# Softmax statistics through DMAs, a second stage 14 units behind, and query casts on GpSimd in a three-group attention layer

## What is computed

```python
qa, ka, va, ga, qb, kb, vb, gb, qc, gc = jnp.split(proj, IN_SPLITS, axis=-1)
# A: 6 heads, causal window of 128, a learned sink per head
oa, _ = banded_attention(qa * scale, ka, va, A_WINDOW - 1, sink)
# B: 6 heads, three (window, dilation) pairs, combined by their softmax denominators
for (win, dil) in ((128, 1), (512, 4), (2048, 16)):
    qs = to_strided(qb * scale, dil)[:, :, :, None, :]
    o, lse = banded_attention(qs, to_strided(kb, dil), to_strided(vb, dil), win // dil, None)
    outs.append(from_strided(o[:, :, :, 0], B, dil).astype(jnp.float32))
    lses.append(from_strided(lse[..., 0], B, dil))
wts = jax.nn.softmax(jnp.stack(lses, axis=0), axis=0)
ob = jnp.sum(wts[..., None] * jnp.stack(outs, axis=0), axis=0)
# C: 4 heads, cross attention into 256 memory tokens
pc = jax.nn.softmax(sc, axis=-1)
```

## Time and profile before

| | |
|---|---|
| median of 3 runs | 2151.43 us (2144.21 to 2152.7) |
| profiled execution | 2152.24 us, of it a span of 2150.1 us from the first to the last instruction |
| TensorE, VectorE, ScalarE, GpSimd busy | 95%, 73%, 63%, 5% of the span |
| mean granted clock of TensorE | 0.973 |
| ten rounds of B (1100.04 to 1499.74 us) | 39.97 us each |
| nine rounds of A (1569.85 to 1689.95 us) | 13.34 us each |

### The profile page before, as it was taken

The page is one execution under the profiler, slowest core; times in us unless marked ns, Lnnn a source line. Parts: engine busy times, 40 slices in busy tenths (PEclk is TensorE's granted clock), DMA queues, the critical chain, the costliest instruction groups (busy, mean ns, idle before and its releaser), DMA issues. The chain is left out here.

```text
span 2150.1 us, 39340 instructions
## 1 busy us (share of the span) xinstructions
PE 2040.4 (95%) x12892; PEld 1717.2 (80%) x12892; DVE 1559.2 (73%) x4410; ACT 1352.9 (63%) x3520; POOL 115.9 (5%) x116
## 2 busy tenths in 40 slices
PE   5999999999999999999889999999999998899998
PEld 4787778888888888888778888887888887688886
DVE  6564674546654574436589999989799997888886
ACT  7454454544555464343699999989699997533333
POOL 1232310000000000002100000000000000000000
PEclk7999999999999999999889999999999999999999
DMA  4466576777577667588876687686779895345543
GB/s 158 152 229 222 177 242 180 217 247 217 155 223 212 225 196 235 184 286 272 201 148 138 130 167 143 131 161 139 150 184 220 227 249 171 98 164 168 176 160 113
DMA packets 351736, 401.40 MB, mean 187 GB/s; under 512 B 105616, under 2 KB 255248, under 8 KB 346688
## 3 DMA queue, kind: packets, MB, share of 16 engines
q1 hardware_dynamic: 343120, 364.80, 62.0%
q0 software_dynamic: 8432, 34.30, 5.2%
HBM read 255.62 MB, written 143.39 MB: 186 GB/s over the span
## 5 line engine op out<-in xcount | busy, mean ns | idle before, releaser
L854 PE MATMUL p_ps<-p_u_hi,p_w_hi 128*128 128x512 f32 x1344 | 534.0, 397 | 26.7 <-DVE p_p_c L739 10.8
L856 PE MATMUL p_ps<-p_u_hi,p_w_lo 128*128 128x512 f32 x1344 | 526.6, 392 | 0.0
L855 PE MATMUL p_ps<-p_u_lo,p_w_hi 128*128 128x512 f32 x1344 | 525.6, 391 | 0.0
L570 DVE TENSOR_TENSOR p_w_lo<-p_w_raw,p_w_hi 128x512 fp32r<-128x512 f32 x336 | 246.6, 734 | 327.0 <-ACT p_w_hi L423 325.4
L1621 ACT ACTIVATE probs<-probs,a_stat 128x256 f32<-128x256 f32 (+1 forms) x896 | 437.4, 497 | 38.9 <-DVE a_stat L1455 36.5
L423 ACT ACTIVATE p_w_hi<-p_w_raw 128x512 fp32r<-128x512 f32 x336 | 211.2, 629 | 329.0 <-PE p_ps L856 304.7
L854 PEld LDWEIGHTS p_ps<-p_u_hi,p_w_hi 128*128 128x128 f32 x1344 | 254.2, 189 | 85.4 <-issue 13.0
L856 PEld LDWEIGHTS p_ps<-p_u_hi,p_w_lo 128*128 128x128 f32 x1344 | 253.7, 189 | 54.4
L855 PEld LDWEIGHTS p_ps<-p_u_lo,p_w_hi 128*128 128x128 f32 x1344 | 254.2, 189 | 50.8
L1455 DVE CUSTOM_DVE_ANT_0 probs<-a_ps_s,fixed 128x256 f32<-128x256 f32 (+1 forms) x704 | 251.9, 398 | 48.3 <-PE a_ps_s L1354 45.7
L1424 PE MATMUL a_ps_t<-fixed,probs 128*128 128x128 f32 x1660 | 262.0, 279 | 23.6 <-ACT a_pT L1645 16.5
(11 more groups left out here) (202 smaller groups left out, 2762.6 us busy)
## 6 DMA issues: line engine op xcount, KB each, us to landing
p_w_raw<-in_w_in SPq DMA_DIRECT2D x156, 256.0 KB, 3.7
p_w_raw<-scratch_w_s SPq DMA_DIRECT2D x144, 256.0 KB, 3.6
scratch_qk_hi<-p_out_a SPq DMA_DIRECT2D x80, 256.0 KB, 4.0
scratch_qk_lo<-p_out_b SPq DMA_DIRECT2D x80, 256.0 KB, 4.1
a_v<-scratch_v SPq DMA_DIRECT2D x40, 512.0 KB, 8.2
scratch_gate<-p_out_a SPq DMA_DIRECT2D x64, 256.0 KB, 3.8
scratch_v<-p_out_a SPq DMA_DIRECT2D x256, 64.0 KB, 2.3
a_gate<-scratch_gate SPq DMA_DIRECT2D x64, 256.0 KB, 6.0
```

The source lines that it names most:

```text
L570: nc.vector.tensor_tensor(w_lo[:, m % 3, :, :], w_raw[:, entry(j, g), :, :], w_hi[:, m % 3, :, :].bitcast(F32), ALU.subtract).then_inc(w_l ...
L854: nc.tensor.matmul(bank, hi, u_hi[j][:, k, :], start=j < 2 and k == 0, stop=False, skip_group_check=True)
L855: nc.tensor.matmul(bank, hi, u_lo[j][:, k, :], start=False, stop=False, skip_group_check=True)
L856: last = nc.tensor.matmul(bank, lo, u_hi[j][:, k, :], start=False, stop=k == KH - 1, skip_group_check=True)
```

## The change

- `TAIL` of B is 14 instead of 18. The exchange stands earlier in the round: slots 1 to 5 and 9, with the far spread in slot 9 and its small matmuls in slot 11 of the round before.
- The statistics of the middle units go another way: GpSimd stores them to DRAM as soon as pair 19 has its sums, waits, and loads them back in four DMAs in the layout that VectorE needs. The middle weights go back the same way. Eight of the eleven small matmuls of a phase and VectorE's four picking instructions are gone. Dependent steps of VectorE stand at different places of a slot, with work between them.
- GpSimd makes all casts: eight in a phase of B, four in one of A. VectorE and ScalarE make none.
- Group A reads its sink without a copy.

```diff
-        return Unit("r4", (c, r), (n, r), P * len(tiles), tiles, r, 16 + 4 * c + r)
+        return Unit("r4", (c, r), (n, r), P * len(tiles), tiles, r, 16 + 4 * r + c)
...
-    TAIL = 18 if kind == "B" else 4
+    TAIL = 14 if kind == "B" else 4
...
-                for b in range(NCH):
-                    last = nc.tensor.matmul(ps_x[:, 128 + 32 * b:160 + 32 * b].rearrange("p (x n) -> p x n", x=2), group4[:, b, :],
-                                            stat[:, s, :, 16:32], start=True, stop=True)
...
-            if kind == "A" and slot == 0:
-                dve.nop(nofuse=True)
-                nc.vector.tensor_copy(sink_now[:, s, :], sink[:, :, bass.ds(h, 1)].rearrange(
-                    "p a o -> p (a o)")).then_inc(sink_ready, 1)
-                dve.wait_ge(sink_ready, p + 1)
...
+            if at == (2, 0):
+                dve.wait_ge(step, done + 1)
+                dve.wait_ge(middle_loaded, 64 * p + 64)
+                nc.vector.tensor_tensor(by_chunk(low), middle[:, 0, :, :], by_chunk(work[:, 0, 0:16]), ALU.min).then_inc(step, 1)
...
+            if kind == "B" and e == 8:
+                dve.wait_ge(middle_back, 64 * p + 64)
...
+    def pool_parts(pool):
+
+        def gather(phase):
+
+            p, s = number(phase), phase[1]
+            pool.wait_ge(sums_ready, p * NP + 20)
+            pool.dma_start(sc["middle_stats"], stat[:, s, 32:64]).then_inc(middle_stored, 16)
+            pool.wait_ge(middle_stored, 32 * p + 16)
+            for b in range(NCH):
+                pool.dma_start(middles[:, 8 * b:8 * b + 8],
+                               sc["middle_stats"][32 * b:32 * b + 32, :].rearrange("j (r e) -> r j e", r=NCH)).then_inc(middle_loaded, 16)
+
+        def give_back(phase):
+
+            p, s = number(phase), phase[1]
+            pool.wait_ge(weights_ready, p + 1)
+            pool.dma_start(sc["middle_weights"], work[:, 7, 16:32]).then_inc(middle_stored, 16)
+            pool.wait_ge(middle_stored, 32 * p + 32)
+            for r in range(NCH):
+                pool.dma_start(coef[:, s, 16 + 4 * r:20 + 4 * r],
+                               sc["middle_weights"][32 * r:32 * r + 32, :].rearrange("j (b c) -> b j c", c=NCH)).then_inc(middle_back, 16)
+
+        def cast(phase):
+
+            p = number(phase)
+            if kind == "B" and p > 0:
+                pool.wait_ge(q_loaded, 32 * p)
+                pool.wait_ge(scores_ready, p * NP)
+                for i in range(4):
+                    nc.gpsimd.tensor_copy(q[:, 1, i * CHUNK:(i + 1) * CHUNK].rearrange("p (b i a) -> p b i a", i=4, a=8),
+                                          by_residue(q[:, 0, :])[:, 4 * i:4 * i + 4, :].rearrange(
+                                              "p i (b a) -> p b i a", a=8).bitcast(F32)).then_inc(q_copied, 1)
+                for g in range(4):
+                    nc.gpsimd.tensor_copy(*natural_piece(g)).then_inc(natural_copied, 1)
...
+        def pool_round(a, c, b, d):
+            if a and a.g.kind == "B":
+                a.parts.cast(a.phase)
+                if c:
+                    c.parts.give_back(c.phase)
+                a.parts.gather(a.phase)
+            elif a and a.g.kind == "A":
+                n = 2 * a.phase[0] + a.phase[1]
+                if n == 0:
+                    a.parts.cast((0, 0))
+                    c.parts.give_back(c.phase)
+                a.parts.cast(((n + 1) // 2, (n + 1) % 2))
```

More of the change, by code:

```diff
@@ L1453, in scores @@
                 a = 2 * P - u.keys
-                start = sink_now[:, s, 1:2] if kind == "A" else 3e38
+                start = sink[:, 1, h:h + 1] if kind == "A" else 3e38
                 last = nc.vector.tensor_tensor_reduce(
@@ new lines, in exchange @@
+            at = (slot, place)
+            done = p * DVE_STEPS
+            far = ps_x[:, 0:32].rearrange("p (x b) -> p x b", x=2)
+            middle = middles.rearrange("p (b x c) -> p x c b", x=2, c=NCH)
+            by_chunk = lambda of: of.rearrange("p (c b) -> p c b", b=NCH)
+            low, ex, inv = work[:, 1, 0:16], work[:, 3, :], work[:, 6, 0:16]
+            if at == (1, 2):
+                dve.wait_ge(max_ready, p * NP + NP)
+                dve.wait_ge(gathered, p + 1)
+                nc.vector.tensor_tensor(work[:, 0, 0:16], far[:, 0, :], near_stat(s, 0), ALU.min).then_inc(step, 1)
@@ L1675, in scalar_parts @@
-        return named(scores=scores, exchange=exchange, copy=copy, keep=keep, copy_queries=copy_queries)
+        return named(scores=scores, exchange=exchange, copy=copy, keep=keep)
+    def pool_parts(pool):
[8 more added lines that the diff above has]
+        def give_back(phase):
+            p, s = number(phase), phase[1]
+            pool.wait_ge(weights_ready, p + 1)
[5 more added lines that the diff above has]
+        def cast(phase):
+            p = number(phase)
+            if kind == "B" and p > 0:
[7 more added lines that the diff above has]
+                    nc.gpsimd.tensor_copy(*natural_piece(g)).then_inc(natural_copied, 1)
+            if kind == "A" and p < 2 * heads:
+                pool.wait_ge(q_loaded, 32 * p + 32)
+                if p < 2:
+                    pool.wait_ge(prev.scores_ready, prev.TOTAL)
+                else:
+                    pool.wait_ge(scores_ready, (p - 1) * NP)
+                for g in range(4):
+                    nc.gpsimd.tensor_copy(*natural_part(p, g)).then_inc(q_copied, 1)
+        return named(gather=gather, give_back=give_back, cast=cast)
@@ L1751, in tensor_round @@
                 if c:
-                    c.parts.exchange(c.phase, i)
+                    c.parts.give_back(c.phase, i)
+                for v in slot.new:
+                    a.parts.gather(a.phase, v)
                 if slot.two_before and slot.two_before[1] % 2:
@@ L1758, in vector_round @@
             for i, slot in enumerate(slots_of(a, c, b, d)):
-                if c and c.g.kind != "B":
-                    c.parts.exchange(c.phase, i)
+                if c:
+                    c.parts.exchange(c.phase, i, 0)
                 if slot.ahead:
@@ L1776, in vector_round @@
                     x.parts.gated(x.phase, e)
-                if c and c.g.kind == "B":
-                    c.parts.exchange(c.phase, i)
+                if c:
+                    c.parts.exchange(c.phase, i, 2)
+                for v in slot.new:
+                    a.parts.spread_far(a.phase, v)
         def scalar_round(a, c, b, d):
```

216 lines of the change are left out of this document (81 added, 135 removed).

## The result

The changed kernel takes 2172.3 us (median of 4 runs, 2170.43 to 2173.61) against 2148.57 for the kernel before in the same session: a ratio of 1.011, 95% interval 1.0084 to 1.0136. It is slower, by 24 us; the forecast was 2135. The profiled execution has a span of 2169.6 us, 19.5 above that of before.

A forecast was written before the change was run, and what follows sets the result against it. VectorE and ScalarE were taken as nearly equal bounds of the attention. From the profiled 2152.2 us, less 12 (B), 2 (A) and 3 (TAIL), with the detour at 0, it forecast 2135 us, range 2128 to 2145.

The forecast's parts named there:

- the detour of the middle statistics: Store and four loads on GpSimd's queue before VectorE's slot 2: 6.7 us, within 8.5, so cost 0.
- The slack: From the sums of pair 19 to the end of slot 1: 9.1 us, 8.5 in a faster round.
- The statistics come late: Rival: VectorE waits at slot 2 for the detour; 2168 us if the chain takes 11.5 us; chance 0.09.
- freed in B, as seen: Casts and picks removed in B free VectorE 2.85, ScalarE 2.1 us a round; 2.1 to 2.4 seen.
- casts beside the scalings, B: In B, VectorE's scalings stand still beside GpSimd's eight casts: 2.0 us lost a round.
- freed in A: Removed casts and sink copy in A free VectorE 1.0 and ScalarE 1.04: 1.0 us a round.
- casts beside the scalings, A: In A, VectorE's scalings stand still beside GpSimd's four casts: 0.8 us lost a round (0.5 to 1.1).
- TAIL 14: Four slots fewer from B to A gain 6.1 us, fuller round 2 costs 2.3; 3 us taken as gain.
- the 0.25 added for TensorE: In B, 0.85 us a round kept by VectorE was raised to 1.1 because TensorE gets ahead meanwhile.
- The lock: VectorE and GpSimd share ports exclusively, so scalings wait for casts: 2.0 us a round in B, 0.8 in A.
- The way back: The middle weights' return has from slot 5 until slot 19, hidden by 14 slots of 1.5 us.
- The issues: Rival: VectorE's scalings hold up GpSimd's DMA issues, making the chain 14.2 us: 2198 us; chance 0.04.

The follow-up runs named there:

- e4_hold_loads: Changed kernel, but SyncE's large key and value loads that start with a round wait until the middle statistics have landed: 2135.51 us, ratio 0.9921.
- e6_hold_tiny_casts: e4_hold_loads, but each GpSimd cast copies only 32 of its 512 columns: 2126.6 us, ratio 0.9891.
- e5_hold_late2: Changed kernel with SyncE's large loads held until the middle statistics have landed, and the exchange two slots later: 2133.96 us, ratio 0.9921.
- e12_detour_only: e4_hold_loads, but all casts back on ScalarE and VectorE in their old slots: 2141.4 us, ratio 0.9958.
- e8_casts_only: Kernel before, with only the attention's casts moved to GpSimd; exchange by matmuls, TAIL 18 and the sink's copy kept: 2170.3 us, ratio 1.0107.
- e11_casts_only_tiny: e8_casts_only, but each GpSimd cast copies only 32 of its 512 columns: 2135.61 us, ratio 0.9913.
- e2_late4: Changed kernel with TAIL 18 and every step of the exchange four slots later: 2171.78 us, ratio 1.0092.
- e1: Changed kernel with the exchange, from the common minimum on, two slots later, TAIL still 14: 2147.62 us, ratio 0.9963.

## Why the prediction was wrong

**The step that failed** is the detour of the middle statistics: "So 2.3 + 4 x 0.53 + 2.3 = 6.7 us, within the 8.5 [...] so I take 0". Its first half was right: undisturbed, the chain takes 6.2 us (four issues at 0.68 instead of 0.53, landing in 2.1). Two things were wrong.

- *The slack.* 8.5 us was read too long, and in the kernel before. The exponential of the earlier trace rows is the last of pair 18. That of pair 19, the 40th of the phase, comes 1.25 us later:

```profile
1250.83 0.51 ACT L1621 ACTIVATE probs<-probs,a_stat 128x256 f32<-128x256 f32 x1
```

  Its sum is there at 1251.4, so the cover was 7.8 us (1251.4 to 1259.2), and 8.7 in the rounds between. VectorE was busy for nearly all of it, among other things with additions and gating of the phase before:

```profile
1253.16 0.87 DVE L1575 TENSOR_TENSOR probs<-a_ps_o,probs 64x256 f32<-64x256 f32 x2
...
1255.27 0.69 DVE L1609 TENSOR_TENSOR a_gate<-probs,a_gate 128x512 f32<-128x512 f32 x1
```

  In the changed kernel these stand at other places of the round. Between the store and the minimum VectorE has only scores, scalings and one small step, and it is ready 6.0 or 7.5 us after the store, in turn, without an idle moment. So even the free chain was about as long as its cover.
- *The queue.* "Nothing large is ahead in this queue now" looked at GpSimd's queue alone. The loads of SyncE's queue pass the same DMA engines, and they start with the new round, just where the detour now lies. The window taken for their idleness, with a share of 0.19, was too short and lay just ahead of those loads. In the rounds with the long waits, the first of them (k_hi) is issued 1.5 us after the sums of pair 19; in the kernel before it came 5.7 to 6.6 us after them. In the changed kernel:

```profile
1276.00:1278.00 2.00, 1.62 (x18) 1.19 (x16) 1.84 (x11) 2.00 (x9) 2.00 (x4) 1.00 1.21 231
...
1282.00:1284.00 2.00, 0.30 (x3) 0.06 (x1) 0.00 (x0) 0.00 (x0) 0.00 (x0) 1.00 1.26 154
1284.00:1286.00 2.00, 0.00 (x0) 0.00 (x0) 1.44 (x11) 0.02 (x1) 0.00 (x0) 0.89 1.21 219
1286.00:1288.00 2.00, 1.50 (x6) 1.34 (x7) 1.86 (x13) 2.00 (x9) 0.00 (x0) 0.50 1.34 203
```

The DMA share is 1.2 and more while the loads are under way (it sums the times of packets, so it passes 1 where they overlap); then all engines stand, and TensorE's clock falls as well. In these two rounds the chain became 12.7 and 9.3 us. This is the rival *The statistics come late*, mechanism and named culprit (the k loads), which had a chance of 0.09 and a price of 2168 us for a chain of 11.5 us. It came out at 2172. The 12.4 us row, a small load behind large ones, pointed the right way, and was dismissed because its large loads were in the same queue.

**The other terms**, read where most of the wait is gone (in the ten rounds 3.5 us of it are left in e4_hold_loads and 6.6 in e6_hold_tiny_casts; removing it altogether, in e5_hold_late2, made a round 0.08 us shorter):

| term | predicted | measured |
|---|---|---|
| round of B | 38.8 us | 38.80 (e4_hold_loads) |
| round of A | 13.1 us | 13.03 |
| freed in B, as seen | 2.1 to 2.4 us a round | 39.97 - 38.48 = 1.5 (e6_hold_tiny_casts) |
| casts beside the scalings, B | 2.0 us | 38.80 - 38.48 = 0.3 |
| freed in A | 1.0 us | 13.34 - 12.56 = 0.8 |
| casts beside the scalings, A | 0.8 us | 12.96 - 12.56 = 0.4 |
| copy of the sink, A | 0.32 us | not seen (13.35 in e12_detour_only, 13.34 before) |
| TAIL 14 | 3 us | 10.6 - 6.3 = 4.3, not run by itself |
| detour | 0 | 37 us (2172.3 - 2135.5), with 13 us of waits left |

TAIL: from the last score of B to the first of the marks of A shown above it is 61.3 us after (1529.61 to 1590.94) and 71.9 before (1497.93 to 1569.85), 10.6 less; from the first score to the last of round 2 it is 56.7 us in e4_hold_loads and 50.4 before, 6.3 more. The rest of the change is in both stretches, in the second also the longest wait left in e4_hold_loads (6.4 us). The forecast of 2135 us is what the kernel takes when SyncE's loads are out of the way (2135.5). In B this is luck: the sum took 2.85 us as freed where 1.5 is seen, and 2.0 as the casts' cost where 0.3 is seen. The two errors, with the 0.25 added for TensorE, nearly cancel: 1.1 us a round was predicted, 1.17 measured. By the prediction's own sign of being wrong, another cost of the lock than 2.0 and 0.8 us a round, this term failed too; it was hidden in the sum.

**The lock** was argued rightly. The scaling does stand still beside a cast: two take 1.09 us (at 1605.27 in A, with GpSimd's casts from 1604.98 on) instead of 0.6. In e4_hold_loads the excess is 21 us in 400, some 2.0 a round as predicted. But only 0.3 of it is seen: VectorE is busy 376.52 of 400 us there and 356.30 in e6_hold_tiny_casts, with nearly equal rounds, so the excess fills time in which it would have been idle. Once the casts have left, VectorE is not the bound, which the sum took it to be; what is, no run here shows. In the kernel before, with the casts alone moved, the same lock costs eight times as much, 2.5 us a round between e8_casts_only and e11_casts_only_tiny (41.97 and 39.51), most of it through the falls of TensorE's clock. Whether TAIL or another difference decides that wasn't tested.

**The way back** of the weights was hidden, as predicted: in the changed kernel its loads land 6.9 us after issue (median), and VectorE never waits for them. In e4_hold_loads it waits once in the ten rounds, 2.8 us at 1100.9.

**The issues** were not starved: 675 to 837 ns with a landing of 2.0 us at best, beside scalings. The Trainium skill (SBUF — State Buffer, section SBUF: two separate sides) warns of about 3100 ns for a DMA that takes 620 alone; no issue of this queue came near it.

## What to carry to other kernels

A small transfer on the path can be late when any queue has large ones under way (here 4.5 us to land instead of 2.1): look for what every queue issues in that stretch, and let what isn't urgent wait for it. A slack read before a change is not the slack after it, since a change that removes or moves work shortens the cover too; lay it out in slots of the new kernel. And casts given to GpSimd beside VectorE's scalings went better in short instructions here: the sum of their time rose from 48 to 82 us, what they held up fell from 21 to 7.

## What the hardware showed that was not expected

- **A scaling can be passed over by a whole row of casts.** By the lock as predicted, a scaling waits for one cast, 0.6 us. In e2_late4 one stood while seven came to their end (4.35 us for one instruction, at 1139.44), and the like came five times in the twelve phases of B, and once in e1, e4 and e5. The Trainium skill (SBUF — State Buffer, section Who interferes with whom) says that the holder keeps the ports for a whole instruction and the other blocks; the rows agree, but who is next when casts follow each other directly it doesn't settle, and here it was at times not VectorE. Four instructions of 128 columns instead of one of 512 left 7 of 21 us of excess. Why a row of short casts lets the scaling in sooner was not tested by itself.
- **Small loads land late behind another queue's large ones.** 4 KB loads on GpSimd's queue: 2.1 us alone, 4.5 in the median and up to 9.7 beside 512 KB loads of SyncE's queue. The Trainium skill (DMA: Bandwidth & Descriptors, section Issuing engines are not separate DMA queues) says that DMAs of different engines end on the same 16 DMA engines and interleave. The times agree with sharing; the interleaving did not keep the small ones short. Whether the size or the number of the large loads decides by how much wasn't tested.
- **A fall of TensorE's clock outlasts what led to it.** In e8_casts_only TensorE was busy 3.7 of the 6 us from 1260 to 1266; the low level then held for 10 to 14 us, and the round was 5 us longer. The kernel before has two shorter ones in its ten rounds (6.8 us each), in rounds of 41.1 instead of 39.3 to 40.1 us. Ten rounds with split casts had one fall. What decides that, and why e8 falls in every second round, stays open.
